# A two-block transformer kernel: the first 128 tokens taken ahead of the second 128 between the mixer and the experts

## The reference, cut to what matters

```
x = x + g1 * rms_norm(y, norm1_post)                 # y: output of the mixer (mix @ w_out)
h = rms_norm(x, norm2_pre) * (1 + sc2) + sh2
q = (h @ wq).reshape(T, 8, 2, 128)                   # 8 heads, two queries of 128 each
s = einsum('thcd,hcnd->thcn', q, subkeys)            # two times 128 scores per head and token
s1, i1 = top_k(s[:, :, 0], 16); s2, i2 = top_k(s[:, :, 1], 16)
sc, ci = top_k(all 256 sums s1 + s2, 16)             # 16 experts per head and token
e = i1[ci // 16] * 128 + i2[ci % 16]; g = softmax(sc)
out = sum over 8 heads and 16 experts of gelu(u[e] . h) * g * v[e]
x = x + g2 * rms_norm(out, norm2_post)
```

## Time and profile before

| | us |
|---|---|
| median of 3 runs (1396.40 to 1398.37) | 1396.42 |
| the profiled execution | 1398.12 |
| its span | 1396.2 |
| TensorE busy | 1168.3 (84%) |
| VectorE busy | 935.9 (67%) |
| ScalarE busy | 504.3 (36%) |
| GpSimd busy | 327.4 (23%) |
| mean DMA rate | 291 GB/s |

### The profile page before, as it was taken

One profiled execution on the slowest core, in us unless ns is written; L12 is line 12 of the kernel. 1 busy time (PEld: TensorE's weight loads), 2 busy tenths in 40 slices (PEclk: granted clock), 3 DMA queues, 4 the chain that ended last, 5 costly groups with the idle time before them and its releaser, 6 DMA issues.

```text
span 1396.2 us, 15468 instructions
## 1 busy us (share of the span) xinstructions
PE 1168.3 (84%) x5486; PEld 821.0 (59%) x5486; DVE 935.9 (67%) x1880; ACT 504.3 (36%) x954; POOL 327.4 (23%) x310
## 2 busy tenths in 40 slices
PE   5889899999538887888888788777867998799999
PEld 4878888998424433434344343333324787699887
DVE  5765687786568677776767776676555675566544
ACT  2544434444433222212222221222123566455432
POOL 4000000000034454444444545445531000000000
PEclk9999999999769999989999999999987999899999
DMA  8743366684169999999999999999993522255551
GB/s 336 280 183 155 121 227 254 230 336 161 59 253 426 427 427 426 427 426 427 427 427 427 426 427 427 426 428 422 426 404 130 183 91 91 91 181 178 185 188 53
DMA packets 57695, 405.66 MB, mean 291 GB/s; under 512 B 6908, under 2 KB 7108, under 8 KB 9108
## 3 DMA queue, kind: packets, MB, share of 16 engines
q0 software_dynamic: 38576, 272.49, 46.5%
q1 hardware_dynamic: 19044, 132.19, 25.6%
HBM read 403.61 MB, written 1.05 MB: 290 GB/s over the span
## 4 chain that ended last, share of the span: by engine, by line
PE 39%; DMA 32%; DVE 16%; ACT 6%; issue 5%; SPq 0%; POOL 0%; POOLq 0%; DVEq 0%; ACTq 0%
DMA gbuf<-in_peer_uv,ei 22%; DMA ring<-in_peer_uv,ei 9%; PE bank L629 7%; PE bank L391 6%; PE bank L392 5%; PE bank L394 5%; DVE gbuf L1523 3%; PE bank L787 2%; PE bank L785 2%; PE bank L786 2%; DVE wlo L1147 2%; ACT whi L801 2%; PE bank L406 2%; PE bank L408 1%; PE bank L407 1%
## 5 line engine op out<-in xcount | busy, mean ns | idle before, releaser
L629 PE MATMUL bank<-gbuf,dg 128*128 128x512 f32 x748 | 357.7, 630 | 105.8 <-ACT dg L990 105.7
L1147 DVE TENSOR_TENSOR wlo<-ring,whi 128x1024 fp32r<-128x1024 f32 x196 | 238.0, 1222 | 176.8 <-ACT whi L801 176.6
L629 PEld LDWEIGHTS bank<-gbuf,dg 128*128 128x128 f32 x748 | 146.8, 201 | 305.0 <-issue 193.6
L1523 DVE CUSTOM_DVE_ANT_0 gbuf<-gbuf,h2t 128x1024 f32<-128x1024 f32 x187 | 228.7, 1225 | 119.9 <-DMA gbuf<-in_peer_uv,ei 119.7
L1791 POOL DMA_INDIRECT gbuf<-in_peer_uv,ei x187 | 219.3, 1173 | 346.4 <-PE bank L629 191.3
L801 ACT ACTIVATE whi<-ring 128x1024 fp32r<-128x1024 f32 x196 | 204.6, 1051 | 114.9 <-PE bank L787 47.7
L982 ACT ACTIVATE za<-za 128x4 f32<-128x4 f32 x64 | 13.1, 205 | 454.9 <-DVE za L1523 454.9
L629 PE MATMUL bank<-ring,dg 128*128 128x512 f32 x276 | 137.8, 646 | 37.6 <-ACT dg L990 37.5
L391 PE MATMUL bank<-hh,whi 128*128 128x256 f32 x448 | 114.7, 293 | 8.8 <-DVE hl L1264 4.9
L629 PEld LDWEIGHTS bank<-ring,dg 128*128 128x128 f32 x276 | 55.7, 207 | 112.5 <-issue 65.0
L391 PE MATMUL bank<-hfh,whi 128*128 128x256 f32 x448 | 116.7, 298 | 0.7 <-ACT hfh L821 0.7
(11 more groups left out here) (344 smaller groups left out, 1682.7 us busy)
## 6 DMA issues: line engine op xcount, KB each, us to landing
ring<-in_weights SPq DMA_DIRECT2D x123, 1024.0 KB, 4.9
gbuf<-in_peer_uv,ei POOLq DMA_INDIRECT x187, 15.3
bcs<-in_b_ada POOLq DMA_DIRECT2D x3, 512.0 KB, 13.2
ring<-in_peer_uv,ei POOLq DMA_INDIRECT x69, 15.7
xs<-in_x SPq DMA_DIRECT2D x2, 512.0 KB, 12.6
nb<-in_norm_post POOLq DMA_DIRECT2D x2, 512.0 KB, 9.6
bcs<-in_norm_g SPq DMA_DIRECT2D x2, 512.0 KB, 5.2
out_x<-xs SPq DMA_DIRECT2D x4, 256.0 KB, 2.1
```

What stands on the lines that cost most here:

```text
L629: r = e.matmul(acc[a][j][:, :], dg[:, i % 4, :], expert_rows(i)[:, 1024 + 512 * j:1536 + 512 * j], start=h == 0 and k == 0, stop=h == 7 an ...
L1147: e.tensor_tensor(l, v, h.bitcast(f32), ALU.subtract).then_inc(*o.inc(s_lov, n + 1))
L1523: e.tensor_tensor_reduce(row, row, h2t[:, ITS[n][0], :], 1.0, 0.0, ALU.mult, ALU.add, za[:, n % 2, i % 16:i % 16 + 1]).then_inc(*o.inc(s_d ...
```

## The change

Half 0 goes through the whole chain before half 1 is taken up:

- TensorE signals when half 0 of the mixer's last product is done (`s_first` 1). ScalarE takes the squares of half 0 then, and those of half 1 after the product.
- The subkeys are transposed and copied directly behind the mixer, before the tokens.
- VectorE's order is: output norm of half 0, second norm of half 0, output norm of half 1, then `route(0)`, then the second norm of half 1, then the splits of chunks WQ0+2 and WQ0+3.
- Queries 0 and 1 and the scores of head 0 are computed for each half by itself, in 48 matmuls of 128 columns per half, into the same two banks.
- The splits of WQ0+2 and WQ0+3 no longer stand beside queries 0 and 1. Queries 2 and 3 and the scores of head 1 follow behind half 1's scores.
- `route(0)` waits for half 0's scores alone. The next two routings are cut in behind dots 4 to 15, no longer 0 to 11; the exponentials of pairs 1 and 2 follow gelus 1 and 3.

The diff, cut to its core (renumbered banks and semaphore counts are left out):

```diff
--- before.py
+++ after.py
@@ in build_program
-    TR = counted(... ("hm", 8), ("h2", 4), ("sk", 4), ...)
+    TR = counted(... ("hm", 8), ("sk", 4), ("h2", 4), ...)
...
-    ROUTE_AT = [2 if i < 12 else int(i >= 16 and i % 16 < 12 and i // 16 + 2 < 16) for i in range(256)]
-    EXP_AFTER = {0: 1, 2: 2} | {4 * n + 1: n + 2 for n in range(1, 14)}
+    ROUTE_AT = [2 if 4 <= i < 16 else int(i >= 16 and i % 16 < 12 and i // 16 + 2 < 16) for i in range(256)]
+    EXP_AFTER = {1: 1, 3: 2} | {4 * n + 1: n + 2 for n in range(1, 14)}
...
+    Q_DONE = {(0, 0): 2, (0, 1): 4} | {(h, a): 2 * h + 4 for h in range(1, 8) for a in range(2)}
+    SC_DONE = {(0, 0): 1, (0, 1): 2} | {(h, a): h + 2 for h in range(1, 8) for a in range(2)}
...
     def ahead(n):
-        return [n + 2] if 0 < n < WQ0 + 2 or WQ0 + 16 <= n < NCH - 2 else []
+        return [n + 2] if 0 < n < WQ0 or WQ0 + 16 <= n < NCH - 2 else []
@@ tensor_program (part: after half a == 0 of the last part of wo1)
+                if a == 0 and first:
+                    r.then_inc(*o.inc(s_first, first))
...
-        for a in range(2):
-            for g in range(2):
-                pb = bank((2, 3, 6, 7)[2 * a + g])
-                e.wait_ge(s_h2s, 2 * a + g + 1)
-                feature_half(h2t[:, a, :], pb, g, "h2", 2 * a + g)
...
         n = load_at["sk", 0]
         e.wait_ge(*arrived(n))
         for g in range(4):
-            pb = bank(g)
+            pb = bank((2, 3, 6, 7)[g])
             transposes(pb, [slot(n)[:, 4 * g + f, :] for f in range(4)], 128, "sk", g)
...
+        def half_scores(h, a, pb, at):
+            for c in range(2):
+                r = e.matmul(pb[:, at + 128 * c:at + 128 * c + 128], qT[:, c, 128 * a:128 * a + 128],
+                             skT[:, 2 * h + c, :], start=True, stop=True)
+            return r
...
-        for h in range(2):
-            query(2 * h)
-            query(2 * h + 1)
-            scores(h)
+        first_q = [split_done(WQ0), split_done(WQ0 + 1)]
+        for a in range(2):
+            for g in range(2):
+                b = (6, 7)[g] if a == 0 else (4, 5)[g]
+                pb = bank(b)
+                e.wait_ge(s_h2s, 2 * a + g + 1)
+                feature_half(h2t[:, a, :], pb, g, "h2", 2 * a + g)
...
+            s_ = slice(128 * a, 128 * a + 128)
+            for c in range(2):
+                hi, lo = first_q[c]
+                pb = banks[c] if a else bank(c)
+                for k in range(8):
+                    e.wait_ge(s_fhi, FHI["h2", 2 * a + k // 4])
+                    e.wait_ge(s_flv, FLV["h2", 2 * a + k // 4])
+                    e.matmul(pb[:, s_], hi[:, k, :], hfh[:, k, s_], start=k == 0, stop=False)
+                    e.matmul(pb[:, s_], hi[:, k, :], hfl[:, k, s_], start=False, stop=False)
+                for k in range(8):
+                    r = e.matmul(pb[:, s_], lo[:, k, :], hfh[:, k, s_], start=False, stop=k == 7)
...
+            pb = bank(2 + a)
             e.wait_ge(s_sk, 4)
+            e.wait_ge(s_q, Q_DONE[0, a])
+            half_scores(0, a, pb, 0).then_inc(*o.inc(s_score, a + 1))
+            frees[2 + a] = ((s_sct, a + 1),)
+        query(2)
+        query(3)
+        scores(1)
@@ scalar_program
+        def tokens_norm(a):
+            e.wait_ge(s_x1, 1 + a)
+            e.activation(h2t[:, a, :], xs[:, a, :], AF.Square, accum_out=sm[:, a:a + 1]) ...
             sqrt(sm[:, 2 + a:3 + a], "h2", a)
             for g in range(2):
+                features_hi(a, g, banks[(6, 7)[g] if a == 0 else (4, 5)[g]], "h2")
+        def first_query(a):
+            s_ = slice(128 * a, 128 * a + 128)
+            for c in range(2):
+                e.wait_ge(s_chunk, WQ0 + c + 1) if a else e.wait_ge(s_first, 2 + c)
+                e.activation(qT[:, c, s_], banks[c][:, s_], AF.Copy).then_inc(*o.inc(s_q, 2 * a + c + 1))
+            e.wait_ge(s_score, a + 1)
+            e.activation(sct[:, 0, 2 * a:2 * a + 2, :], banks[2 + a][:, 0:256] ..., AF.Copy) ...
...
+        e.wait_ge(s_first, 1)
+        output_square(0)
+        sqrt(sm[:, 122:123], "y1", 0)
+        e.wait_ge(s_chunk, WQ0)
+        output_square(1)
...
+        tokens_norm(0)
+        sqrt(sm[:, 126:127], "y1", 1)
+        first_query(0)
+        tokens_norm(1)
+        hi(WQ0 + 2)
+        first_query(1)
+        hi(WQ0 + 3)
...
+        route_exp(0)
+        query(2)
+        query(3)
+        scores(1)
@@ vector_program
+        output_norm(0)
+        tokens_norm(0)
+        output_norm(1)
...
-        for g in range(2):
-            for m in ahead(chunk_at["wq", g]):
-                lo(m)
         for _ in route(0):
             pass
+        tokens_norm(1)
+        lo(WQ0 + 2)
+        lo(WQ0 + 3)
         rt, n_rt = route(1), 1
```

More of the change, by code:

```diff
@@ L181, in counted @@
         return at
-    TR = counted(("p0", 1), ("x", 4), ("gates", 1), ("p1", 1), ("hm", 8), ("h2", 4), ("sk", 4), ("h3", 4), ("qk2", 4),
+    TR = counted(("p0", 1), ("x", 4), ("gates", 1), ("p1", 1), ("hm", 8), ("sk", 4), ("h2", 4), ("h3", 4), ("qk2", 4),
                  ("h4", 4))
@@ L395, in product, with part @@
             r.then_inc(*o.inc(s_chunk, n + 1))
-        def part(name, j, c, two, xh, xl_, start, stop, by_k=None):
+        def part(name, j, c, two, xh, xl_, start, stop, by_k=None, first=None):
             n = chunk_at[name, 2 * j + c]
@@ L408, in part, with token_product @@
                     r = e.matmul(two[a][:, :], xl_[:, k, s_], hi[:, kk, :], start=False, stop=stop and kk == 1)
+                if a == 0 and first:
+                    r.then_inc(*o.inc(s_first, first))
             r.then_inc(*o.inc(s_chunk, n + 1))
-        def token_product(name, b0, b1, xh, xl_, by_k=None):
+        def token_product(name, b0, b1, xh, xl_, by_k=None, first=None):
             two = [bank(b0), bank(b1)]
             for i in range(4):
-                part(name, i // 2, i % 2, two, xh, xl_, i == 0, i == 3, by_k)
+                part(name, i // 2, i % 2, two, xh, xl_, i == 0, i == 3, by_k, first if i == 3 else None)
         def feature_half(src, pb, g, *mark):
@@ L579, in tensor_program @@
         token_product("wo0", 4, 5, hh, hl, mix_ready)
[L580 removed]
+        token_product("wo1", 0, 1, hh, hl, first=1)
         frees[4], frees[0] = ((s_y1, 1),), ((s_y1, 2),)
         frees[5], frees[1] = ((s_y1, 3),), ((s_y1, 4),)
[L585 to L590 removed]
         n = load_at["sk", 0]
@@ L598, in scores @@
         def scores(h):
             pb = bank(3)
-            e.wait_ge(s_sk, 4)
-            e.wait_ge(s_q, 2 * h + 2)
-            for a in range(2):
-                for c in range(2):
-                    r = e.matmul(pb[:, 256 * a + 128 * c:256 * a + 128 * c + 128], qT[:, c, 128 * a:128 * a + 128],
-                                 skT[:, 2 * h + c, :], start=True, stop=True)
-            r.then_inc(*o.inc(s_score, h + 1))
-            frees[3] = ((s_sct, h + 1),)
-        def h2_ready(k):
-            g = k // 4
-            for a in range(2):
-                e.wait_ge(s_fhi, FHI["h2", 2 * a + g])
-                e.wait_ge(s_flv, FLV["h2", 2 * a + g])
@@ L615, in query @@
-        def query(g):
-            product("wq", g, g % 3, hfh, hfl, None if g else h2_ready)
-            frees[g % 3] = ((s_q, g + 1),)
-        for h in range(2):
-            query(2 * h)
-            query(2 * h + 1)
-            scores(h)
+            e.wait_ge(s_q, Q_DONE[h, 1])
+            half_scores(h, 0, pb, 0)
+            half_scores(h, 1, pb, 256).then_inc(*o.inc(s_score, SC_DONE[h, 1]))
+            frees[3] = ((s_sct, SC_DONE[h, 1]),)
+        def query(g):
+            product("wq", g, g % 3, hfh, hfl)
+            frees[g % 3] = ((s_q, g + 3),)
@@ L937, in scalar_program, with output_square @@
         for i in range(4):
-            taken("wo1", i)
-        for a in range(2):
+            for m in ahead(chunk_at["wo1", i]):
+                hi(m)
+        def output_square(a):
             e.activation(jks[a][:, H2[1]], banks[a][:, :], AF.Square, accum_out=sm[:, 121 + 4 * a:122 + 4 * a]).then_inc(
                 *o.inc(s_nsq, SQ["y1", 2 + a]))
-            sqrt(sm[:, 122 + 4 * a:123 + 4 * a], "y1", a)
-        e.wait_ge(s_x1, 2)
-        e.wait_ge(s_chunk, WQ0)
-        e.wait_ge(*o.now)
-        for a in range(2):
+        def tokens_norm(a):
+            e.wait_ge(s_x1, 1 + a)
             e.activation(h2t[:, a, :], xs[:, a, :], AF.Square, accum_out=sm[:, a:a + 1]).then_inc(*o.inc(s_nsq, SQ["h2", a]))
@@ L1418, in vector_program @@
         for i in range(4):
-            taken("wo1", i)
+            for m in ahead(chunk_at["wo1", i]):
+                lo(m)
         def normed_add(a, mark, pair, gain, junk, at):
@@ L1431, in normed_add, with output_norm, tokens_norm @@
             e.tensor_tensor(xs[:, a, :], xs[:, a, :], junk, ALU.add).then_inc(*o.inc(s_x1, at))
-        for a in range(2):
+        def output_norm(a):
             e.wait_ge(s_nsq, SQ["y1", 2 + a])
             normed_add(a, ("y1", a), (banks[4 + a], banks[a]), bc[0], jks[a], 1 + a)
```

(7 more changed lines are left out.)

36 lines of the change are left out of this document (21 added, 15 removed).

## The result

| | before | after |
|---|---|---|
| median, runs on the same chip (8 each) | 1396.53 | 1400.16 |
| range of these runs | 1395.50 to 1398.37 | 1399.10 to 1401.42 |
| the profiled execution | 1398.12 | 1400.18 |
| its span | 1396.2 | 1398.2 |

The ratio after to before is 1.0023, with a 95% interval of 1.0012 to 1.0034: 3.6 us slower by the medians. That is inside the range that was predicted (1385.5 to 1401) and on its wrong side: 1393.2 was forecast, 3.2 faster.

A forecast was written before the change was run, and what follows sets the result against it. The prediction took DMA bytes to bound the expert stage. An earlier first gather (-12.2), moved transfers (+9.0) and no gaps (0) summed to -3.2 us, 1393.2 on the median of 1396.42, range 1385.5 to 1401.

The forecast's parts named there:

- The bound and the shape of the sum: Expert stage: it ends when its bytes have moved, so an earlier first gather gains and bytes behind it cost.
- The start of the first query: Query 0 on half 0 was to start at 366.3, when the first split of its tokens ends.
- From the end of the query to routing: Copy, scores and score copy between query and routing 0: 1.6 us in place of 2.37.
- The time of one narrow matmul: Queries 0 and 1: each 128-column matmul takes 0.12 us at full clock, no gain from half the columns.
- Rival 1: Half-width matmuls of queries 0 and 1 run like plain float32, 0.24 us each: 1403.2 us, chance 0.13.
- 40 at 0.12 if the clock rises: Half 0's queries: 8 matmuls cold at 0.21, then 40 at 0.12, ending 373.1; 17 cold if later, ending 374.5.
- So no gap, with 2.9 us to spare: Expert stage: gathers never run dry while buffers are freed; 2.9 us of cover left, each further microsecond costs one.
- partly cold: Half 1's 48 query matmuls, from 389.8, run partly at half clock; score copy done at 398.5.
- Rival 3: Gather supply gaps open because wq 2 lands after 409 or VectorE takes longer: 1396.3 us, no change, chance 0.13.
- The transfers, +9.0: Norm rows, wq 2 and wq 3, 3.15 MB moved behind the first gather, cost 9.0 us, between 7.4 and 9.9.
- Rival 2: The transfers moved behind the first gather cost nothing or little, so -9 to -12 us: 1386, chance 0.14.
- The sum: Whole kernel: earlier first gather -12.2, moved transfers +9.0, gaps 0, together -3.2 us.

The follow-up runs named there:

- e1_wide: The changed kernel with each half-width matmul of queries 0 and 1 moving its 128 columns twice, 256 in all: 1391.36 us, ratio 0.9953 to the kernel before.
- e9_dots2: The changed kernel with dots 0 to 3, gelu 0 and their combinations moved earlier, chunk wq 4's rounding copy directly behind gelu 0: 1396.03 us, ratio 0.9994.
- e8_late: The kernel before, with the loads of wq 2, the two norm rows and wq 3 held until routing 0's indices are there: 1403.19 us, ratio 1.0050.
- e4_clock: The changed kernel, 128 columns kept, with 16 and 40 unused 512-column matmuls put in front of half 0 and half 1: 1392.72 us, ratio 0.9978.

## Why the prediction was wrong

**The bound and the shape of the sum: right.** The stage ends when its bytes have moved, so an earlier first gather is gained and what moves behind it is lost. That account with a third term for holes gives the end of all twelve traces above.

**The start of the first query: right.** Predicted 366.3, that is 9.2 behind the product; it came 9.2 behind it (364.99 against 355.76). VectorE's queue, the squares and the subkey transposes cost what was said. From the end of the query to routing also went as said, but for the clock.

**The time of one narrow matmul: right.** 0.12 was taken, the same as for 256 columns; 0.11 was measured at the full clock and 0.213 at the half one. Rival 1 with its 0.24 at the full clock is false, though its slower side is where the result fell. By the Trainium skill, "TensorE: Matmul & The Clock Gate", section "Back-to-back issue gap", it would have been 81 ns; this case's 111 ns are for four-byte weights and lie nearer to the 256-column spacing of 119 ns.

**"40 at 0.12 if the clock rises": this is the step that failed.** It put 8 to 17 of the 48 matmuls at the half clock, from the rise that the trace of before shows inside 378 to 379. All 48 ran at it. So the first gather came 31.6 behind the product in place of 28.2: -8.8 and not -12.2. e1_wide shows that the width of these matmuls decides it: same weights, same count, same point of the program, and the clock rises 2.3 us into the stream. The assumption was hidden in my own reasoning. I had argued that columns don't matter for the spacing, and took it to hold for the clock as well.

The rise that was carried over did not come under 256-column matmuls. The timeline of before has these at 379.44 and later; inside 378 to 379 TensorE was at its transposes of the subkeys, of 128 columns in plain float32:

```profile
377.00 2.68 PE L376 MATMUL bank<-ident,ring 128*128 128x128 f32 x16
```

So the clock rose under one kind of 128-column instruction and not under another, the single-pass float32r product, at about the same spacing (0.22 and 0.21). The number of columns alone is not the rule.

**"So no gap, with 2.9 us to spare": fell with it.** Half 1 pays for the clock again. Its score copy ended at 405.04 (404.66 and 0.38), 49.3 behind the product, where the prediction had 41.4; gather 11 came 68.2 behind it and not 59.9, 8.3 late. 3.4 of that also delayed the gathers themselves; the other 4.9 ate the spare 2.9. The transfers were cheaper by 1.6, which let the supply end sooner by as much. 4.9 + 1.6 - 2.9 = 3.6 us of holes would follow, and 4.4 were measured. The text did say what the spare time was and that each further microsecond costs one; it did not carry the cold second stream into it beyond "partly cold". Rival 3 had the symptom, but not the cause: wq 2 landed at 409 (issued at 391.35, 17.7 to land), 6.9 ahead of ScalarE's copy of it at 415.93. e9_dots2 shows that the holes were the price that the account gives them: closing them was worth 4.1.

**The transfers, +9.0: too dear by 1.6 to 2.7.** Bytes give 7.4, e8_late 7.0 and its trace 6.3. The engine time of idle engines was the wrong measure: beside gathers the same packets cost no more than their bytes. The prediction's use of the Trainium skill, "DMA: Bandwidth & Descriptors", section "Issuing engines are not separate DMA queues", held: e8_late shows the other queue's bytes at their full price in the gathers' time. Rival 2, for which they were free, is false.

**The sum.** -12.2 + 9.0 + 0 = -3.2 was predicted; -8.8 + 7.4 + 4.4 = +3.0 was found. The error of 6.2 is +3.4 from the late first gather, -1.6 from the transfers and +4.4 of holes. The clock made the first and, through half 1, most of the last; but 1.6 of the holes in the working above are the cheaper transfers' earlier end, so their saving came to nothing. With the clock as assumed the forecast would have been near: e1_wide, where it rises, is 1391.36 against the predicted 1393.2.

What stays open: why a dense stream of narrow float32r matmuls does not raise the clock, where transposes of 128 columns did. Only 128 and 256 columns at one spacing were run, so where between them the change lies, and which trait of an instruction decides, is not told.

## What to carry to other kernels

Halving the columns of these float32r matmuls bought next to no time (0.11 in place of 0.12 us apart at the full clock, 0.21 in either case at the half one), and it kept a low clock low: a product that is split for an early start should keep its width, or the engine should go into it at the full clock. In a stage bound by DMA bytes, add up three terms for its end: when its first transfer starts, which bytes move behind that start (bytes over rate), and whether the consumers free the first buffers before the supply in hand has run out. A cost counts only while it is the one that ends last: taking half of the bytes away was worth nothing with the hole open and 3.6 us with it closed.

## What the hardware showed that I had not expected

- 128-column float32r matmuls, back to back: TensorE 10.54 of 11 us busy, and the granted clock stayed 0.50; with 256 columns at the same spacing of 0.213 it rose 2.3 us after the stream began. In the kernel before it rose, inside 378 to 379, under plain float32 transposes of 128 columns. With the clock up the narrow stream held it, 0.11 apart, up to 370 in e4_clock.
- A DMA share of 0.98 beside 375 GB/s in place of 427: the share of queue time hides holes that the rate shows.
- A 1 MB weight tile took 17.7 us to land behind two norm rows and beside gathers, and still cost the stage no more than its bytes.
